# The first gate tiles in two column groups: token columns ahead of the shift rows, two shift columns behind the norm sum

## The reference

```python
def adaln(cond, w, b):
    m = jax.nn.silu(cond) @ w + b
    return m.reshape(cond.shape[0], 1, N_MOD, D_MODEL)

def modulate(x, g, shift, scale):
    return rmsnorm(x, g) * (1.0 + scale) + shift

def ffn_half(x, m, j, g, wg, wu, wd):
    return x + 0.5 * m[:, :, j + 2] * swiglu(modulate(x, g, m[:, :, j], m[:, :, j + 1]), wg, wu, wd)
```

## Time and profile before

| | us |
|---|---|
| median of 3 runs | 2596.72 |
| the three runs | 2593.45, 2596.72, 2596.87 |
| profiled execution, its own time | 2597.37 |
| its span, first to last instruction | 2596.1 |
| PE busy | 2535.7 (98%) |
| PE weight loads busy | 2431.8 (94%) |
| DVE busy | 1664.2 (64%) |
| ACT busy | 1141.6 (44%) |
| POOL busy | 940.7 (36%) |

### The profile page before, as it was taken

How to read it: one execution, slowest core, us unless ns; L and a number is a source line. 1 busy time by engine, 2 the same in 40 slices (tenths; PEclk the granted TensorE clock), 3 DMA queues, 4 the chain that set the end, 5 groups by cost and what they waited for, 6 DMA issues and landing times. The chain is left out here.

```text
span 2596.1 us, 44830 instructions
## 1 busy us (share of the span) xinstructions
PE 2535.7 (98%) x18603; PEld 2431.8 (94%) x18603; DVE 1664.2 (64%) x2584; ACT 1141.6 (44%) x1945; POOL 940.7 (36%) x649
## 2 busy tenths in 40 slices
PE   6999999999988999999999999999999999999998
PEld 5999999999766999999999999999999999999998
DVE  5865757624677677676767767676464557757484
ACT  4442424442566454333445433344432546434253
POOL 2433434443200343434344343434332224443342
PEclk8999999999999999999999999999999999999999
DMA  7334434321100223424322343432312112232222
GB/s 272 127 134 147 142 135 143 106 91 51 60 1 1 98 66 128 150 98 165 122 89 82 130 147 98 169 122 76 101 54 69 59 43 73 66 94 70 82 78 78
DMA packets 204049, 260.36 MB, mean 100 GB/s; under 512 B 4932, under 2 KB 158152, under 8 KB 203848
## 3 DMA queue, kind: packets, MB, share of 16 engines
q1 hardware_dynamic: 203176, 254.88, 29.3%
q10 hardware_dynamic: 672, 2.62, 0.3%
HBM read 253.66 MB, written 3.82 MB: 99 GB/s over the span
## 5 line engine op out<-in xcount | busy, mean ns | idle before, releaser
L2413 POOL TENSOR_TENSOR wl<-raw,wh 128x512 fp32r<-128x512 f32 x324 | 471.5, 1485 | 703.9 <-ACT wh L2503 601.1
L2503 ACT CAST wh<-raw 128x2048 fp32r<-128x2048 f32 (+1 forms) x102 | 173.7, 1703 | 318.0 <-PE psU L3164 277.4
L2442 POOL TENSOR_TENSOR wl<-wsum,wh 128x512 fp32r<-128x512 f32 x72 | 94.1, 1307 | 353.0 <-ACT wh L2579 353.0
L2834 DVE SCALAR_TENSOR_TENSOR x<-psG,hgate,x 128x128 f32<-128x128 f32 (+1 forms) x232 | 88.4, 435 | 167.0 <-PE psG L3164 167.0
L3287 PE MATMUL psG<-sum_h,wh 128*128 128x320 f32 x576 | 178.9, 311 | 1.1
L2438 POOL TENSOR_TENSOR wl<-raw,wh 128x512 fp32r<-128x512 f32 x72 | 104.5, 1451 | 202.0 <-ACT wh L2588 202.0
L3290 PE MATMUL psG<-sum_h,wl 128*128 128x320 f32 x576 | 177.6, 308 | 0.0
L3289 PE MATMUL psG<-sum_l,wh 128*128 128x320 f32 x576 | 177.6, 308 | 0.0
L3289 PE MATMUL psU<-sum_l,wh 128*128 128x320 f32 x576 | 177.6, 308 | 0.0
L3290 PE MATMUL psU<-sum_h,wl 128*128 128x320 f32 x576 | 177.6, 308 | 0.0
L3287 PE MATMUL psU<-sum_h,wh 128*128 128x320 f32 x576 | 177.5, 308 | 0.0
(11 more groups left out here) (699 smaller groups left out, 7678.4 us busy)
## 6 DMA issues: line engine op xcount, KB each, us to landing
mraw<-in_mod_w SPq DMA_DIRECT2D x64, 1024.0 KB, 7.2
raw<-in_ffn_w_gate SPq DMA_DIRECT2D x44, 1024.0 KB, 5.1
raw<-in_ffn_w_up SPq DMA_DIRECT2D x44, 1024.0 KB, 5.1
raw<-in_ffn_w_down SPq DMA_DIRECT2D x48, 768.0 KB, 4.4
raw<-in_odd_w_in SPq DMA_DIRECT2D x12, 1024.0 KB, 5.2
raw<-in_even_w_in SPq DMA_DIRECT2D x9, 1024.0 KB, 5.1
raw<-in_ffn_w_down SPq DMA_DIRECT2D x8, 1024.0 KB, 5.0
mscale<-in_mod_w SPq DMA_DIRECT2D x4, 1024.0 KB, 10.7
```

The source lines that it names most:

```text
L2413: ins = nc.gpsimd.tensor_tensor(wl[:, slot, piece], raw[:, slot, piece], wh[:, slot, piece].bitcast(F32), ALU.subtract)
L2442: nc.gpsimd.tensor_tensor(part1(f, wl, 3), part1(f, wsum, 3), part1(f, wh, 3).bitcast(F32), ALU.subtract).then_inc(block_plo, 1)
L2503: nc.scalar.copy(wh[:, slot, 0:width], raw[:, slot, 0:width]).then_inc(w_hi, 1)
L2834: ins = nc.vector.scalar_tensor_tensor(out=xt, in0=src, scalar=hg_of(i * 2 + m, c), in1=xt, op0=ALU.mult, op1=ALU.add)
```

## The change

PE's list alone changes, and one constant that DVE reads. Tile 0 and tile 1 of the first gate pair are each cut into two column groups: 640 token columns (a matmul of 384 and one of 256) and two shift columns (a matmul of two). PE's new order is: sums and turns of the scale block; shift sums for k 0 to 3; the wait for the gate pair's low weights; token columns of tile 0, each k behind its `hl`; shift sums for k 4 to 7; token columns of tile 1; turns of the shift block; the norm sum; the wait for the shift columns of `hl`; the two shift columns of tile 0 and of tile 1, 24 matmuls each, with the semaphore of the finished tile behind each; the up tiles. Since tile 1's bank is in use when the shift is turned, one of the turned columns' four banks is another for block 1 (`psU[:, 1]`). All other engines' lists stand as they were.

```diff
-    HEAD_BANKS = (psA, psB, psG[:, 2, :], psU[:, 2, :])
+    HEAD_BANKS = ((psA, psB, psG[:, 2, :], psU[:, 2, :]), (psA, psB, psU[:, 1, :], psU[:, 2, :]))
...
-                ins = nc.vector.tensor_tensor(mod[:, :, col], HEAD_BANKS[g][:, 0:4].rearrange("p (t c) -> p c t", c=2),
+                ins = nc.vector.tensor_tensor(mod[:, :, col], HEAD_BANKS[b][g][:, 0:4].rearrange("p (t c) -> p c t", c=2),
...
+        def head_sums(b, ks=range(DT)):
+            for k in ks:
+                if k % 2 == 0:
+                    pe.wait_ge(head_in[b][k // 2], 16)
+                for g in range(4):
+                    ins = nc.tensor.matmul((psG, psU)[b][32 * g:32 * g + 2, 0, 0:2 * P], cs[:, k],
+                                           (mscale, mshift)[b][:, k, g * 2 * P:(g + 1) * 2 * P], start=k == 0, stop=k == DT - 1)
+            if ks[-1] == DT - 1:
+                ins.then_inc(head_mm, 1)
+
+        def head_turns(b):
+            for side in range(2):
+                pe.wait_ge(mrow_ok[side], b + 1)
+            for t in range(DT):
+                rows_g = slice(32 * (t // 2), 32 * (t // 2) + 2)
+                ins = nc.tensor.transpose(HEAD_BANKS[b][t // 2][:, t % 2 * 2:t % 2 * 2 + 2],
+                                          mrow[rows_g, b, t % 2 * P:(t % 2 + 1) * P], ident[rows_g, rows_g])
...
+        def first_gate(slot, mods_done):
+
+            def tokens(m):
+                return (((SH, SH + 384), psG[:, 1 + m, SH:SH + 384]), (WIDE_B, psG[:, 0, m * 256:(m + 1) * 256]))
+
+            def token_split(k):
+                pe.wait_ge(z_lo, k + 1)
+
+            unit_tile(slot, 0, DT, wide(hh), wide(hl), tokens(0), True, True, token_split)
+            head_sums(1, range(4, DT))
+            unit_tile(slot, 1, DT, wide(hh), wide(hl), tokens(1), True, True)
+            head_turns(1)
+            norm_sum(0, mods_done)
+            pe.wait_ge(sh_lo, 1)
+            for m in range(2):
+                unit_tile(slot, m, DT, wide(hh), wide(hl), (((0, SH), psG[:, 1 + m, 0:SH]),), True, True).then_inc(gate_mm, 1)
...
             for i in range(HEAD_PAIRS):
                 t = old_tiles(f) + 2 * i
+                if f == 0 and i == 0:
+                    head_sums(1, range(4))
                 slot = unit_in(base, 0, i)
...
-                unit_tile(slot, 0, DT, wide(hh), wide(hl), wide_of(psG, 0), True, True,
-                          h_ready(r) if i == 0 else None).then_inc(gate_mm, 1)
-                if i == 0:
-                    norm_sum(r, mods_done)
+                if f == 0 and i == 0:
+                    first_gate(slot, mods_done)
                 else:
...
-        for b, w in enumerate((mscale, mshift)):
...
+        head_sums(0)
+        head_turns(0)
```

More of the change, by code:

```diff
@@ L3215, in mod_rows_turn @@
             turn(psB[:, 0:P], macc[:, 0, 0:P]).then_inc(mturn_ok, 2)
+        def head_sums(b, ks=range(DT)):
[14 more added lines that the diff above has]
+                                          mrow[rows_g, b, t % 2 * P:(t % 2 + 1) * P], ident[rows_g, rows_g])
+            if b:
+                ins.then_inc(mturn_ok, MOD_HEAD)
+            else:
+                ins.then_inc(head_turn, 1)
+        def first_gate(slot, mods_done):
[11 more added lines that the diff above has]
+                unit_tile(slot, m, DT, wide(hh), wide(hl), (((0, SH), psG[:, 1 + m, 0:SH]),), True, True).then_inc(gate_mm, 1)
         def norm_sum(r, mods_done):
@@ L3233, in ffn @@
                 passed(pe, res_ok[0], res_before[f"ffn{f}"])
-                unit_tile(slot, 0, DT, wide(hh), wide(hl), wide_of(psG, 0), True, True,
-                          h_ready(r) if i == 0 else None).then_inc(gate_mm, 1)
-                if i == 0:
-                    norm_sum(r, mods_done)
-                else:
-                    mod_rows_turn(f, 0, 0)
-                    mod_rows(f, 0, 1)
-                unit_tile(slot, 1, DT, wide(hh), wide(hl), wide_of(psG, 1), True, True).then_inc(gate_mm, 1)
+                if f == 0 and i == 0:
+                    first_gate(slot, mods_done)
+                else:
+                    unit_tile(slot, 0, DT, wide(hh), wide(hl), wide_of(psG, 0), True, True,
+                              h_ready(r) if i == 0 else None).then_inc(gate_mm, 1)
+                    if i == 0:
+                        norm_sum(r, mods_done)
+                    else:
+                        mod_rows_turn(f, 0, 0)
+                        mod_rows(f, 0, 1)
+                    unit_tile(slot, 1, DT, wide(hh), wide(hl), wide_of(psG, 1), True, True).then_inc(gate_mm, 1)
                 slot = unit_in(base, 1, i)
```

## The result

The changed kernel takes 2612.44 us (median; 2611.55 to 2614.05) against 2596.80 us before in the same measurement: a ratio of 1.0062, 95% interval 1.0045 to 1.0080. It is **slower by 15.6 us**, where 9 had been forecast.

What follows compares the result with a forecast made beforehand. PE bounds the kernel, a row of matmuls. Norm sum 9.2 us later, a tile of 7.1 to 7.3 less, 5.3 of small matmuls, 1.9 for the clock: +9.1 on 2596.72, forecast 2606, range 2600.5 to 2612.5.

Steps and rivals of the forecast that it cites:

- rival 1: Stream of two-column matmuls does not bring PE's clock up: up tile +15.4 us, end 2612; chance 0.12.
- What comes earlier: First gate tile's token columns no longer wait for the shift: begin about 31.85 instead of 40.05, end 39.7 us.
- The second half of the shift sums: Behind tile 0's token columns on PE: 16 matmuls at 0.057, 0.9 us, to 40.6.
- What comes later: Shift transposes 9.2 us later; DVE and ACT work queued behind moves too: norm sum at 60.1, PE idle about 12 us.
- What is added: Behind the norm sum: 48 two-column matmuls, each with its own weight load, 0.11 us each, 5.3 us at full clock.
- Rival 2: Small matmuls' weight loads run at half the price, 0.057 us: +6.5 us, 2603, or +4.6, 2601; chance 0.13.
- The clock: Half clock after the 12 us gap, full again 3.8 us after PE resumes, among the small matmuls: costs 1.9 us.
- an up tile past 72: Start of the up tile, forecast near 68.3 us; past 72 would mean the small matmuls never bring the clock up.
- To the end: From the up tile on, PE runs almost without waits, so the whole +9.1 us was carried to the end.
- Rivals 3 and 4: Not slower, adds done under tile 1: 2592 or 2595, chance 0.06; a later stage swallows the delay: some 2599, chance 0.09.
- rival 3: Norm sum does not wait for the transposes, adds of squares done under tile 1: 2592 or 2595; chance 0.06.

Runs made afterwards that it cites:

- adds_first: Changed kernel with ACT's six squares and DVE's six adds put ahead of the shift rows and the up weights' cast; ratio to the kernel before 1.0002.
- wide_shift: Changed kernel with the 48 two-column shift matmuls widened to 128 columns, the further ones token columns computed again; ratio to the kernel before 1.0054.
- wide_shift_256: Changed kernel with the 48 two-column shift matmuls widened to 256 columns, the further ones token columns computed again; ratio to the kernel before 1.0052.
- filled_gap: Changed kernel with 66 matmuls of 384 columns into an unused bank between the turns and the norm sum; ratio to the kernel before 1.0053.

## Why the prediction was wrong

The direction and its cause were right; the size was not. The measured median, 2612.44, stands at the very end of the range; taken by the ratio from the 2596.72 us shown it is 2612.8, just past 2612.5. That the range reaches so far is owed to rival 1, not to the forecast. Step by step:

- **What comes earlier** was right: tile 0 from 31.71 (forecast 31.85) to 39.6 (39.7), the clock rising in it as the sums alone had brought it up before.
- **The second half of the shift sums** was mis-sized: 0.9 us forecast, 1.84 measured (39.61 to 41.45). I divided 3.63 us by the 64 records of the scale block and counted 16 matmuls; each of these matmuls leaves two records, and the half block shows x32. That is 0.9 of the 7 us missing, and the count could have been read in the earlier trace rows: one transfer's two k, eight matmuls, stand there as x16.
- **What comes later** was right, and is what decided: adds_first shows it, where moving the adds, and the squares and the cast ahead of them on ACT, turned the 11.90 us of waiting into 0.58. The distance of 11.9 from bias add to norm sum held to 0.1 us. The norm sum came at 60.95 (forecast 60.1), late by the sums' 0.9.
- **What is added** was right at the clock it was worked out for: 0.111 us (adds_first) for the 0.11 taken from the earlier trace rows. Rival 2, loads at half the price, is out. One reading behind it was off and did no harm: the ten records of the earlier trace rows are five matmuls (L3423 runs once for each 128 of the 640 tokens), two records each, so 0.11 is the price of one load; a matmul of the 48 leaves one record and has one load. The Trainium skill, "TensorE: Matmul & The Clock Gate", "Back-to-back issue gap", has about 25 ns as the floor of an isolated small matmul; none of the 48 comes near it, the closest start 0.111 us apart. The Trainium skill, "TensorE: Matmul & The Clock Gate", "LDWEIGHTS (loading the stationary operand)", has P/1.2 ns for a load, 107 ns for 128 columns; the 111 at full clock agrees, and at half clock the runs show 213.
- **The clock** is the step that failed. It was to come back 3.8 us after PE resumed, as it had in the first gate tile. It stayed at half through the whole stream (10.45 us for 6.2 forecast, 4.25 of the missing 7) and into the up tile (1.9 more). That is rival 1, priced at +15.4 and 2612, given 0.12, and its sign, an up tile past 72, came (73.34). I set it low because the clock had risen under the shift sums with pauses between them, and took that PE at work is enough. The runs show that it isn't: matmuls of 2 or 128 columns, each behind a load of 0.213 us, brought no rise in over 10 us (the change, wide_shift), those of 256 columns did within 2.4 us of the stream's start and 4.3 of the norm sum's (wide_shift_256).
- **To the end** was right: the delay of 16 us at the up tile is still 15.8 at 2130 us. Rivals 3 and 4 are out; adds_first, which does what rival 3 supposed, came out at no change, not 2 to 5 us faster, because of the clock again.

Sum of the misses: 0.9 + 4.25 + 1.9 = 7.05, and 9.1 + 7.05 = 16.1 against 16.05 read in the trace. Why the clock falls in such a stream, or does not rise, is not settled by these runs beyond which streams did it; what in a matmul's work the clock's grant goes by was not measured.

## What to carry to other kernels

When a step is moved back in one engine's list, look in the other engines' lists at what is queued behind its result: here six adds that had nothing to do with the shift, with a cast and six squares ahead of them on ACT, kept PE waiting for 11.9 us because they stood behind it. Columns that are cut off from a wide matmul pay a full weight load each; at full clock three cost 0.33 us in either place that was tried. Slip them in between wide ones, where the clock stayed in full, and not as a stream of their own, where it fell and three cost 0.64.

## What the runs showed of the hardware

A PE that waits for nothing can lose its clock. In adds_first and filled_gap a stream of two-column matmuls began at full clock and was at half after 4.3 and 2.8 us; at half it never recovered within the stream, which lasted 10.45 us in the change. The Trainium skill, "TensorE: Matmul & The Clock Gate", "HAM oscillation — how this bites in real kernels", puts the fall down to gaps in which PE is idle. Here the trace shows none (windows of adds_first, busy 4.00 of 4.00; by starts, which are not modelled, no two matmuls of the stream are over 0.22 us apart), so that rule is not the whole of it. Nor are such streams the only place: in the kernel before the clock also fell near 2115.8 under matmuls of 384 and 256 columns, 1.2 us behind a wait of 1.92 us, and did not in the changed kernel behind the same wait. An idle PE held its clock longer than before: it fell 4.5 us behind the turns (49.0 to 53.5), where it had fallen 1.5 to 2 us behind the last sums in the kernel before. And 48 matmuls of 256 columns took less time than 48 of two, 8.95 against 12.39 us with the norm sum ahead of them, because they brought the clock back.
